# Sample cross attention on four column groups of the array: each head multiplied on its own 32 columns, one softmax over 128 rows

## The chip, the cores and the metric

The kernel runs on one core of a Trainium2 chip. The metric is the device time of one execution in microseconds. Before the change the median of three runs is 3585.67 us (3581.64 to 3586.48).

## What is computed

Two layers of a decoder trunk, for a prompt of 1024 tokens and for 8 samples of one new token each, which share the weights. In each layer a token mixer, a cross attention to 256 memory tokens and a gated MLP with a short convolution add to the residual. The change is in the cross attention of the samples. The prompt has keys and values that the layer computes; every sample has its own, from a cache in HBM:

```python
def cross_attention(h, mk, mv, w_xq_l, w_xo_l):
    q = (h @ w_xq_l).reshape(B, L, X_HEADS, X_HEAD_DIM)          # 4 heads of 256
    s = jnp.einsum('bqhd,bmhd->bhqm', q, mk) * (X_HEAD_DIM ** -0.5)
    p = jax.nn.softmax(s, axis=-1)
    o = jnp.einsum('bhqm,bmhd->bqhd', p, mv)
    return o.reshape(B, L, D_MODEL) @ w_xo_l
```

For the samples `h` is 8 x 1 x 1024, and `mk` and `mv` are 8 x 256 x 4 x 256 of float32: one MB of keys and one MB of values for each sample and layer.

## The kernel before, in words

Activations lie transposed, with features on the 128 partitions: `xT`, `Y`, `hh` and `hl` are 128 x 8 x 1032, the last 8 columns being the samples. Each weight slab (128 x 1024, 512 KB) is loaded into a ring of two buffers (`w_raw`), split by ScalarE into a high part (L235) and by GpSimd into the rest (L243), and kept in one of three places. A product with weights is three multiplications (L258 to L260). `stage_cross_ffn` writes every engine's order out by hand, and the engines meet at semaphores.

Cross attention has three stages on TensorE. The prompt's scores, turns and values come first, with the output projection of the first 384 columns, `unit(0, i)`. Then come `unit(1, 0)` to `unit(1, 7)`, the output projection of the next 384 columns, 24 multiplications of 384 columns each; the samples' attention lies between these. Then `unit(2, i)` takes the last 264 columns, which hold the 8 samples, so that `unit(2, 0)` waits for the samples' output (`s_lo`).

The samples' attention goes in this order.

- SyncE (`caches`, L2031) loads 16 pieces of one MB, t = 0 to 7 the keys and t = 8 to 15 the values of the samples, in turn into the two buffers `mem_keys` and `mem_values`. Piece t waits until TensorE is done with piece t-2 (`s_done`). After pieces 4, 6, 8, 10 and 12 it loads a weight slab.
- VectorE clears `probs` (L2497) and puts the samples' queries into it (L2499), with 32 columns for each sample and feature block, one of which isn't zero.
- `sample_scores(t)` (L2147) multiplies 8 feature blocks, 32 stationary columns and 256 moving columns, one after another into the same 32 rows (row 8h+b of bank 0, so that all heads and samples share 32 rows). Two samples follow each of `unit(1, 0)` to `unit(1, 3)`.
- Softmax over 32 rows: VectorE takes the maximum (L2507, L2508), ScalarE the exponential (L2345), VectorE clears the first 528 columns of `probs` (L2509) and divides (L2512, L2513). `unit(1, 4)` covers this. `sample_turn` (L2154) transposes the rows, VectorE copies them into `probs` (L2517), `unit(1, 5)` covers that.
- `sample_values(t)` (L2166) makes 4 multiplications of 512 moving columns into 32 rows of two banks. t = 8, 9, 10 come before `unit(1, 6)`, t = 11 to 15 after it, then `mean(1)` (L2110) and `unit(1, 7)`.
- ScalarE copies the 32 x 1024 result (L2353) beside `unit(1, 7)`, `sample_out` (L2174) turns it with 8 transposes, ScalarE and VectorE split it into high and low part (L2358, L2526), and `unit(2, 0)` goes on.

A float32 multiplication shows as two records in the trace, so L2147 has 256 records for 128 multiplications.

Elsewhere in the kernel smaller tiles of the array are used as well: the prompt's window attention puts its values (L485) on two groups of 64 columns in turn, and the samples' window attention (L1459) too.

Of the kernel before, what the change touches and what calls it, by code (L numbers as in the profile page):

```python
# [11 lines left out]
ALU = mybir.AluOpType  # L12
ACT = mybir.ActivationFunctionType
AX = mybir.AxisListType

P = 128
D = 1024
SEQ = 1024
NS = 8
T = SEQ + NS  # L20
# [3 lines left out]
KT = D // P  # L24
# [9 lines left out]
NMEM = 256  # L34
XH = 4
# [116 lines left out]
def build_program(nc, io):  # L152
    ctx = ExitStack()
    with ctx:
# [32 lines left out]
        Y = sb("Y", [P, KT, T])  # L187
# [3 lines left out]
        rs = sb("rs", [P, T])  # L191
        gT = sb("gT", [P, DEPTH, N_GROWS])
        cT = sb("cT", [P, DEPTH, 4, 2 * FT])
        ident = sb("ident", [P, P])
# [10 lines left out]
        ps = ctx.enter_context(nc.psum_tensor("ps", [P, 8, 512], F32))  # L205
# [6 lines left out]
        act_c, dve_c, pe_c, pool_c = (Chain(lasting_sem(n)) for n in ("act_step", "dve_step", "pe_step", "pool_step"))  # L212
# [1537 lines left out]
        def stage_cross_ffn(l, mkT, mv_tile, memory):  # L1750
# [6 lines left out]
            with ExitStack() as ph:  # L1757
                def tmp(name, shape, dt=F32):
                    return ph.enter_context(nc.sbuf_tensor(f"{name}{l}", shape, dt))

                probs = tmp("x_probsT", [P, KT * 264])
                acc, sq, rt = tmp("x_acc", [P, 2, 384]), tmp("x_sq", [P, 2, 384]), tmp("x_rt", [P, 2, 384])
                S = [t.rearrange("p (j k) -> p j k", j=2) for t in (rs[:, 0:512], rs[:, 512:1024], tmp("x_scores", [P, 512])[:])]
                small = tmp("x_small", [P, 4, 4, 2])
                rows, st = probs[0:32, 600:856], tmp("xs_stat", [32, 4])
                PT = probs[:, 0:2048].rearrange("p (a h q) -> p a h q", a=2, h=XH)
                qm = probs[:].rearrange("p (k c) -> p k c", k=KT)
                qm_at = probs[:].rearrange("p (k b c) -> p k b c", k=KT, b=NS)
                pm = probs[:, 0:528].rearrange("p (a c) -> p a c", a=2)
                pm_at = probs[:, 0:528].rearrange("p (a b c) -> p a b c", a=2, b=NS)[:, :, :, 0:32]\  # L1770
                    .rearrange("p a b (h e) -> p a b h e", e=8)[:, :, :, :, 0]
                o_rows = probs[0:32, 1024:2048]
                flat = [t[:].rearrange("p k t -> p (k t)") for t in (mkT, mv_tile)]
                mv = flat[1].rearrange("p (a f) -> p a f", a=2)
                s = {n: sem(f"x_{n}") for n in (
# [4 lines left out]
                scale = 256 ** -0.5  # L1780
# [35 lines left out]

                def new_values(bank):

                    t = ps[:, bank, 0:288].rearrange("p (h c) -> p h c", h=XH)[:, :, 0:64]
                    return t.rearrange("p h (d e) -> p h d e", d=2)[:, :, :, 0:NS]  # L1820

                def by_head(t):
                    return t.rearrange("p (h d) b -> p h d b", d=2)
# [20 lines left out]
                class End:  # L1844
# [7 lines left out]
                    s = {n: sem(f"e_{n}") for n in ("sq", "sum", "root", "x", "hh", "hl", "rs", "norm", "whole", "tree", "mean")}  # L1852
# [204 lines left out]
                def tensor(pe):  # L2057
# [32 lines left out]
                    def unit(c, i):  # L2090
                        u = KT * c + i
                        m = LOAD_OF[VISIT[l, "xo", xo_slab(u), c]]
                        wait_low(pe, m)
                        pe.wait_ge(s["out_lo"], (16, 24, 32)[c])
                        if c == 2:
                            pe.wait_ge(s["s_lo"], 1)
                        if u >= 2:
                            pe.wait_ge(s["out"], u - 1)
                        for j in range(KT):
                            w = slice(P * j, P * j + P)  # L2100
                            last = mm3(ps[:, 6 + u % 2, 0:C3[c][1]], w_hi[:, SLOT[m], w], w_lo[:, SLOT[m], w],
                                       hh[:, j, cols(c)], hl[:, j, cols(c)], j == 0, j == KT - 1)
                        last.then_inc(w_used, 1)
# [37 lines left out]
                    def sample_scores(t):  # L2141
                        if t == 0:
                            pe.wait_ge(s["q_ready"], 1)
                        pe.wait_ge(kv_in[t % 2], 16 * (t // 2 + 1))
                        keys = cache(t).rearrange("p (k t) -> p k t", k=KT)
                        for k in range(KT):
                            last = nc.tensor.matmul(ps[0:32, 0, 0:NMEM], qm[:, k, 32 * t:32 * t + 32], keys[:, k, :],  # L2147
                                                    start=(t == 0 and k == 0), stop=(t == NS - 1 and k == KT - 1))
                        last.then_inc(s["s_done"], 1)

                    def sample_turn():
                        pe.wait_ge(s["p_r"], 1)
                        for a in range(2):
                            last = nc.tensor.transpose(ps[:, 1, 32 * a:32 * a + 32], rows[:, P * a:P * a + P], ident[0:32, 0:32])  # L2154
                        last.then_inc(s["pT"], 1)

                    def sample_values(t):
                        b = t - NS
                        if b == 0:
                            pe.wait_ge(s["pm"], 1)  # L2160
                            pe.wait_ge(s["out_lo"], 32)
                        pe.wait_ge(kv_in[t % 2], 16 * (t // 2 + 1))
                        v = cache(t).rearrange("p (a f) -> p a f", a=2)
                        for a in range(2):
                            for h in range(2):
                                last = nc.tensor.matmul(ps[0:32, 4 + h, :], pm[:, a, 32 * b:32 * b + 32],  # L2166
                                                        v[:, a, 512 * h:512 * h + 512],
                                                        start=(b == 0 and a == 0), stop=(b == NS - 1 and a == 1))
                        last.then_inc(s["s_done"], 1)

                    def sample_out():
                        pe.wait_ge(s["o_rows"], 1)
                        for k in range(KT):
                            last = nc.tensor.transpose(ps[:, 1, 32 * k:32 * k + 32], o_rows[:, P * k:P * k + P], ident[0:32, 0:32])  # L2174
                        last.then_inc(s["o_turned"], 1)

                    for u in range(3):
# [16 lines left out]
                    unit(1, 4)  # L2194
                    sample_turn()
                    unit(1, 5)
                    for t in (8, 9, 10):
                        sample_values(t)
                    unit(1, 6)
                    for t in (11, 12, 13, 14, 15):  # L2200
                        sample_values(t)
                    mean(1)
                    unit(1, 7)
                    sample_out()
                    unit(2, 0)
                    mean(2)
# [41 lines left out]
                def scalar(act):  # L2248
# [79 lines left out]
                    for u in range(n):  # L2328
# [5 lines left out]
                        if u >= 9:  # L2334
# [7 lines left out]
                    high(0, range(KT))  # L2342
                    evacuate(1, 3)
                    act.wait_ge(s["neg_r"], 1)
                    nc.scalar.activation(rows[:], ps[0:32, 0, 0:NMEM], ACT.Exp, bias=st[:, 1:2], scale=scale,  # L2345
                                         accum_out=st[:, 2:3]).then_inc(s["exp_r"], 1)
                    squares(0, range(4))
                    evacuate(1, 4)
                    squares(0, range(4, KT))
                    evacuate(1, 5)  # L2350
                    evacuate(1, 6)
                    act.wait_ge(s["s_done"], 2 * NS)
                    nc.scalar.activation(o_rows.rearrange("p (h f) -> p h f", h=2), ps[0:32, 4:6, :], ACT.Copy)\  # L2353
                        .then_inc(s["o_rows"], 1)
                    root(1)
                    evacuate(1, 7)
                    act.wait_ge(s["o_turned"], 1)
                    nc.scalar.activation(by_head(hh[:, :, SEQ:T]), new_values(1), ACT.Copy).then_inc(s["s_hi"], 1)  # L2358
                    evacuate(2, 0)
# [53 lines left out]
                def vector(dve):  # L2413
# [81 lines left out]
                    add(("post", 0, KT - 1))  # L2495
                    dve.wait_ge(s["pv"], 32)
                    dve_c(nc.vector.memset(probs[:], 0.0))  # L2497
                    for h in range(XH):
                        last = nc.vector.tensor_copy(qm_at[:, 2 * h:2 * h + 2, :, 8 * h], Y[:, 2 * h:2 * h + 2, SEQ:T])  # L2499
                    last.then_inc(s["q_ready"], 1)  # L2500
                    normalise(0)
                    add(("post", 1, 1))
                    residual(0)
                    add(("post", 1, 2))
                    add(("post", 1, 3))
                    dve.wait_ge(s["s_done"], NS)
                    dve_c(nc.vector.tensor_reduce(st[:, 0:1], ps[0:32, 0, 0:NMEM], AX.X, ALU.max))  # L2507
                    nc.vector.tensor_scalar(st[:, 1:2], st[:, 0:1], -scale, None, ALU.mult).then_inc(s["neg_r"], 1)  # L2508
                    dve_c(nc.vector.memset(probs[:, 0:528], 0.0))  # L2509
                    low(0, range(0, 4))  # L2510
                    dve.wait_ge(s["exp_r"], 1)
                    dve_c(nc.vector.reciprocal(st[:, 3:4], st[:, 2:3]))  # L2512
                    nc.vector.tensor_scalar(rows[:], rows[:], st[:, 3:4], None, ALU.mult).then_inc(s["p_r"], 1)  # L2513
                    low(0, range(4, KT))
                    adds(0, range(1, 4))
                    dve.wait_ge(s["pT"], 1)
                    nc.vector.tensor_copy(pm_at, ps[:, 1, 0:64].rearrange("p (a h b) -> p a b h", a=2, h=XH))\  # L2517
                        .then_inc(s["pm"], 1)
                    add(("post", 1, 4))
                    adds(0, range(4, KT))  # L2520
# [263 lines left out]
```

## Time and profile before

| | us |
|---|---|
| median of three runs (lowest, highest) | 3585.67 (3581.64, 3586.48) |
| profiled execution, first to last instruction | 3580.1 |
| TensorE busy in it | 3358.2 (94%) |
| VectorE, ScalarE, GpSimd busy | 2316.4, 1186.1, 677.1 |
| mean granted TensorE clock | 0.985 |

For the profiled execution the profile gives the span alone and no separate time; it is 5.6 us below the median of the runs. The engine rows name a line, an engine, an operation and what it writes and reads. PE is TensorE's multiplication, PEld its weight load, DVE is VectorE, ACT ScalarE, POOL GpSimd, SPq the queue of SyncE that issues DMAs. Layer 0's cross attention lies at 820 to 1010 us, layer 1's some 1778 us later.

### The profile page before, as it was taken

What the parts mean: (1) busy time and instruction counts of PE and PEld (TensorE: products, weight loads), DVE (VectorE), ACT (ScalarE), POOL (GpSimd) and SP (SyncE); (2) the same over time, 40 slices, a digit from 0 to 9 for tenths busy, and PEclk for the clock granted to TensorE, in tenths of its full rate; (3) what the DMA queues carried; (4) which work ended last, traced back from release to release, by engine and by line L of the source; (5) the groups of instructions that cost most, each with busy time, mean ns of one, the idle gap of its engine ahead of it and who ended that gap; (6) DMA issues with size and microseconds to landing.
All of it is one profiled execution on the core that took longest, in us unless ns stands there. A gap on an engine that the chain in (4) does not pass through costs nothing. (4 is left out here: it accounts for less than half of the span.)

```text
span 3580.1 us, 50156 instructions
## 1 busy us (share of the span) xinstructions
PE 3358.2 (94%) x20988; PEld 3141.1 (88%) x20988; DVE 2316.4 (65%) x3517; ACT 1186.1 (33%) x1849; POOL 677.1 (19%) x274
## 2 busy tenths in 40 slices
PE   7999889899999999999989998898999999999997
PEld 7999769788599999999889997698876999999996
DVE  6766783733467677776786667736434777676776
ACT  5342363433332222212344324533433221222222
POOL 1111131012221212122111111211113121212120
PEclk9999999999999999999999999999999999999998
DMA  4111223203311111111121122322143111111111
GB/s 171 43 42 61 74 86 124 74 30 141 142 58 42 48 42 54 42 48 44 50 79 43 43 63 72 106 107 76 36 153 134 42 42 48 48 42 48 42 58 50
DMA packets 71168, 245.76 MB, mean 69 GB/s; under 512 B 7968, under 2 KB 22560, under 8 KB 65824
## 3 DMA queue, kind: packets, MB, share of 16 engines
q1 hardware_dynamic: 70656, 242.50, 19.9%
q8 instruction: 166, 2.72, 0.3%
q14 instruction: 58, 0.48, 0.0%
q10 hardware_dynamic: 288, 0.06, 0.0%
HBM read 214.20 MB, written 23.04 MB: 66 GB/s over the span
## 5 line engine op out<-in xcount | busy, mean ns | idle before, releaser
L258 PE MATMUL ps<-hh,w_hi 128*128 128x344 f32 (+2 forms) x4320 | 1417.5, 328 | 105.2 <-issue 26.1
L260 PE MATMUL ps<-hh,w_lo 128*128 128x344 f32 (+2 forms) x4320 | 1389.6, 322 | 0.0
L259 PE MATMUL ps<-hl,w_hi 128*128 128x344 f32 (+2 forms) x4320 | 1389.3, 322 | 0.0
L243 POOL TENSOR_TENSOR w_lo<-w_raw,w_hi 128x1024 fp32r<-128x1024 f32 x270 | 676.9, 2509 | 2840.4 <-ACT w_hi L235 2840.4
L258 PEld LDWEIGHTS ps<-hh,w_hi 128*128 128x128 f32 x4320 | 821.0, 190 | 142.9 <-issue 86.8
L259 PEld LDWEIGHTS ps<-hl,w_hi 128*128 128x128 f32 x4320 | 820.7, 190 | 3.0 <-issue 0.9
L260 PEld LDWEIGHTS ps<-hh,w_lo 128*128 128x128 f32 x4320 | 820.3, 190 | 0.0
L2581 DVE TENSOR_TENSOR Y<-Y,ps 128x344 f32<-128x344 f32 x912 | 432.9, 512 | 156.3 <-PE ps L260 156.3
L235 ACT ACTIVATE w_hi<-w_raw 128x1024 fp32r<-128x1024 f32 x296 | 310.3, 1052 | 438.4 <-PE ps L260 385.6
L2377 ACT ACTIVATE f_c<-f_u,cT 128x1032 f32<-128x1032 f32 (+1 forms) x92 | 111.3, 1212 | 670.0 <-DVE f_u L2546 663.4
L259 PE MATMUL ps<-f_glo,w_hi 128*128 128x344 f32 x960 | 308.1, 321 | 0.0
L260 PE MATMUL ps<-f_ghi,w_lo 128*128 128x344 f32 x960 | 307.6, 320 | 0.0
L258 PE MATMUL ps<-f_ghi,w_hi 128*128 128x344 f32 x960 | 306.1, 319 | 0.0
L2554 DVE SCALAR_TENSOR_TENSOR f_c<-f_u,cT,f_c 128x1024 f32<-128x1024 f32 x172 | 225.2, 1309 | 98.6 <-ACT f_c L2377 95.6
L258 PEld LDWEIGHTS ps<-f_ghi,w_hi 128*128 128x128 f32 x960 | 181.3, 189 | 0.0
L260 PEld LDWEIGHTS ps<-f_ghi,w_lo 128*128 128x128 f32 x960 | 180.6, 188 | 0.0
L259 PEld LDWEIGHTS ps<-f_glo,w_hi 128*128 128x128 f32 x960 | 180.3, 188 | 0.0
L2546 DVE TENSOR_TENSOR f_u<-ps,rs 128x1032 f32<-128x1032 f32 x86 | 105.7, 1229 | 98.8 <-PE ps L260 98.5
L2556 DVE SCALAR_TENSOR_TENSOR f_c<-f_cache,cT,f_c 128x8 f32<-128x8 f32 x172 | 123.6, 719 | 6.2
L1594 DVE TENSOR_TENSOR oq_acc<-oq_acc,oq_sq 128x384 f32<-128x384 f32 (+1 forms) x84 | 43.3, 515 | 96.7 <-ACT oq_sq L1519 92.2
L2393 ACT ACTIVATE f_ghi<-f_c 128x1032 fp32r<-128x1032 f32 x42 | 44.9, 1068 | 149.6 <-DVE f_c L2562 149.6
L258 PE MATMUL ps<-mem_hi,w_hi 128*128 128x256 f32 x256 | 76.7, 300 | 17.6 <-DVE mem_lo L634 10.5
(355 smaller groups left out, 3912.6 us busy)
## 6 DMA issues: line engine op xcount, KB each, us to landing
w_raw<-in_w_stream SPq DMA_DIRECT2D x296, 512.0 KB, 3.3
out_y_cols<-xT SPq DMA_DIRECT2D x9, 1376.0 KB, 5.7
xT<-out_y_cols SPq DMA_DIRECT2D x2, 4128.0 KB, 14.2
mem_keys<-in_cache_mem_k SPq DMA_DIRECT2D x8, 1024.0 KB, 4.8
mem_values<-in_cache_mem_k SPq DMA_DIRECT2D x8, 1024.0 KB, 4.9
mem_keys<-in_cache_mem_v SPq DMA_DIRECT2D x8, 1024.0 KB, 4.7
mem_values<-in_cache_mem_v SPq DMA_DIRECT2D x8, 1024.0 KB, 5.0
xT<-in_x_cols SPq DMA_DIRECT2D x3, 1376.0 KB, 11.5
```

The lines of the kernel that those rows point to most:

```text
L235: nc.scalar.activation(w_hi[:, SLOT[m], :], w_raw[:, m % RR, :], ACT.Copy).then_inc(hi_done, 1)
L243: nc.gpsimd.tensor_tensor(w_lo[:, SLOT[m], :], w_raw[:, m % RR, :], w_hi[:, SLOT[m], :].bitcast(F32), ALU.subtract).then_inc(lo_done["pool ...
L258: nc.tensor.matmul(out, whi, mhi, start=start, stop=False)
L259: nc.tensor.matmul(out, whi, mlo, start=False, stop=False)
L260: return nc.tensor.matmul(out, wlo, mhi, start=False, stop=stop)
L1594: nc.vector.tensor_tensor(a, a, sq[:, j % 2, 0:C3[c][1]], ALU.add).then_inc(acc_used, 1)
L2377: nc.scalar.activation(C[:, h, at], U[:, h, 2 + at.start:2 + at.stop], ACT.Identity, bias=cT[:, l, 3, col:col + 1], scale=cT[:, l, 2, col: ...
L2393: nc.scalar.activation(gh[:, j % 2, :], C[:, 1, :], ACT.Copy).then_inc(f_gh, 1)
L2546: nc.vector.tensor_tensor(tokens3(U[:, h, 2:2 + T]), ps[:, 3 * h:3 * h + 3, 0:CH], tokens3(rs[:]), ALU.mult).then_inc(f_up, 1)
L2554: dve_c(nc.vector.scalar_tensor_tensor(c[:, 0:SEQ], U[:, h, t:t + SEQ], w, c[:, 0:SEQ], ALU.mult, ALU.add))
L2556: dve_c(nc.vector.scalar_tensor_tensor(c[:, SEQ:T], ca[:, col, t, :], w, c[:, SEQ:T], ALU.mult, ALU.add))
L2581: nc.vector.tensor_tensor(y, y, b, ALU.add).then_inc(f_y, 1)
```

## The change

Each head gets its own 32 columns of the array and so its own 32 rows of PSUM. For the scores, the outer loop goes over the two feature blocks of a head (`d`) and the inner over the four heads, so that four multiplications in a row write to rows 0, 32, 64 and 96 of bank 0. Softmax is over 128 rows. Two transposes of 128 x 128 take the place of two of 32 x 128. For the values each head multiplies 256 columns (8 multiplications of 256 instead of 4 of 512) into its 32 rows of bank 4. The result is 128 x 256, `sample_out` is 2 transposes instead of 8. The zeros in `probs` are kept, so the second clearing falls away, and the queries are placed by one copy instead of four. The rows lie in `x_scores` instead of `probs`. The values are placed anew: t = 8, 9 after `unit(1, 5)`, 10, 11 after `unit(1, 6)`, then `mean(1)` and `unit(1, 7)`, then 12 to 15 and `sample_out` right behind them. ScalarE's copy of the result comes after `root(1)` and `evacuate(1, 7)`. The loads are as before.

```diff
+                rows, o_rows, st = third[:, 0:256], third[:, 256:512], tmp("xs_stat", [P, 4])
-                pm = probs[:, 0:528].rearrange("p (a c) -> p a c", a=2)
-                o_rows = probs[0:32, 1024:2048]
+                one_at = probs[:].rearrange("p (k b c) -> p k b c", k=KT, b=NS)[:, :, :, 0]
...
+                def sample_cols(k, b):
+                    return qm[:, k, 32 * b:32 * b + 32]
+                def head_rows(h):
+                    return slice(32 * h, 32 * h + 32)
...
-                        for k in range(KT):
-                            last = nc.tensor.matmul(ps[0:32, 0, 0:NMEM], qm[:, k, 32 * t:32 * t + 32], keys[:, k, :],
-                                                    start=(t == 0 and k == 0), stop=(t == NS - 1 and k == KT - 1))
+                        for d in range(2):
+                            for h in range(XH):
+                                k = 2 * h + d
+                                last = nc.tensor.matmul(ps[head_rows(h), 0, 0:NMEM], sample_cols(k, t), keys[:, k, :],
+                                                        start=(t == 0 and d == 0), stop=(t == NS - 1 and d == 1))
...
-                            last = nc.tensor.transpose(ps[:, 1, 32 * a:32 * a + 32], rows[:, P * a:P * a + P], ident[0:32, 0:32])
+                            last = nc.tensor.transpose(ps[:, 1, P * a:P * a + P], rows[:, P * a:P * a + P], ident[:])
...
                         for a in range(2):
-                            for h in range(2):
-                                last = nc.tensor.matmul(ps[0:32, 4 + h, :], pm[:, a, 32 * b:32 * b + 32],
-                                                        v[:, a, 512 * h:512 * h + 512],
+                            for h in range(XH):
+                                last = nc.tensor.matmul(ps[head_rows(h), 4, 0:256], sample_cols(XH * a + h, b),
+                                                        v[:, a, 256 * h:256 * h + 256],
                                                         start=(b == 0 and a == 0), stop=(b == NS - 1 and a == 1))
...
-                        for k in range(KT):
-                            last = nc.tensor.transpose(ps[:, 1, 32 * k:32 * k + 32], o_rows[:, P * k:P * k + P], ident[0:32, 0:32])
+                        for d in range(2):
+                            last = nc.tensor.transpose(ps[:, 1, P * d:P * d + P], o_rows[:, P * d:P * d + P], ident[:])
...
                     unit(1, 5)
-                    for t in (8, 9, 10):
-                        sample_values(t)
+                    sample_values(8)
+                    sample_values(9)
                     unit(1, 6)
-                    for t in (11, 12, 13, 14, 15):
-                        sample_values(t)
+                    sample_values(10)
+                    sample_values(11)
                     mean(1)
                     unit(1, 7)
+                    for t in (12, 13, 14, 15):
+                        sample_values(t)
                     sample_out()
...
                     evacuate(1, 6)
-                    act.wait_ge(s["s_done"], 2 * NS)
-                    nc.scalar.activation(o_rows.rearrange("p (h f) -> p h f", h=2), ps[0:32, 4:6, :], ACT.Copy)\
-                        .then_inc(s["o_rows"], 1)
                     root(1)
                     evacuate(1, 7)
+                    act.wait_ge(s["s_done"], 2 * NS)
+                    nc.scalar.activation(o_rows, ps[:, 4, 0:256], ACT.Copy).then_inc(s["o_rows"], 1)
...
-                    for h in range(XH):
-                        last = nc.vector.tensor_copy(qm_at[:, 2 * h:2 * h + 2, :, 8 * h], Y[:, 2 * h:2 * h + 2, SEQ:T])
-                    last.then_inc(s["q_ready"], 1)
+                    nc.vector.tensor_copy(one_at, Y[:, :, SEQ:T]).then_inc(s["q_ready"], 1)
...
-                    dve_c(nc.vector.memset(probs[:, 0:528], 0.0))
```

## Rows read from the trace of the kernel before

**Rows 1.** The page: span, busy time of each engine.
```profile
span 3580.1 us, 50156 instructions
PE 3358.2 (94%) x20988; PEld 3141.1 (88%) x20988; DVE 2316.4 (65%) x3517; ACT 1186.1 (33%) x1849; POOL 677.1 (19%) x274
```

**Rows 2.** Stretches, both layers: scores, then values to `unit(2, 0)`. Start:end, length, engines, clock, DMA.
```profile
860.41:901.68 41.27, 41.27 (x201) 26.18 (x200) 10.85 (x6) 14.39 (x22) 11.68 (x4) 1.00 0.59 216
901.68:954.42 52.74, 47.45 (x173) 24.37 (x173) 16.52 (x27) 11.98 (x23) 2.35 (x1) 1.00 0.47 176
2638.60:2679.90 41.30, 41.30 (x201) 26.18 (x200) 10.86 (x6) 14.63 (x23) 11.69 (x4) 1.00 0.59 217
2679.90:2732.86 52.96, 47.65 (x175) 24.32 (x173) 16.52 (x27) 11.98 (x23) 2.35 (x1) 1.00 0.47 176
```

**Rows 3.** TensorE in order of time, layer 0: start, length, line, tiles.
```profile
860.41 3.64 PE L2147 MATMUL ps<-mem_keys,x_probsT 128*32 128x256 f32 x16
863.89 3.62 PE L2147 MATMUL ps<-mem_values,x_probsT 128*32 128x256 f32 x16
867.44 0.44 PE L258 MATMUL ps<-hh,w_hi 128*128 128x384 f32 x1
...
871.56 0.33 PE L260 MATMUL ps<-hh,w_lo 128*128 128x384 f32 x1
871.83 3.64 PE L2147 MATMUL ps<-mem_keys,x_probsT 128*32 128x256 f32 x16
...
906.09 0.30 PE L2154 MATMUL ps<-ident,x_probsT 32*128 32x32 f32 x2
...
910.73 3.62 PE L2166 MATMUL ps<-mem_keys,x_probsT 128*32 128x512 f32 x8
...
919.13 3.62 PE L2166 MATMUL ps<-mem_keys,x_probsT 128*32 128x512 f32 x8 [1.35 <-DMA mem_keys<-in_cache_mem_v]
...
952.73 0.68 PE L2174 MATMUL ps<-ident,x_probsT 32*128 32x32 f32 x8
954.42 0.36 PE L258 MATMUL ps<-hh,w_hi 128*128 128x264 f32 x1 [1.02 <-DVE hl L2526]
```

**Rows 4.** TensorE in order of time: two groups of 64 columns used in turn.
```profile
438.23 1.08 PE L485 MATMUL ps<-xT,rs 128*64 128x256 f32 x8
578.67 1.10 PE L1459 MATMUL ps<-ws_probsT,ws_values 128*64 128x4 f32 x32
```

**Rows 5.** SyncE's queue, values of layer 0: issue, length of issue, what is loaded.
```profile
914.38 0.33 SPq L2031 DMA_DIRECT2D mem_keys<-in_cache_mem_v  x1
914.75 0.43 SPq L226 DMA_DIRECT2D w_raw<-in_w_stream  x1
```

**Rows 6.** A piece alone, issue to landing; and the stretch of three transfers queued.
```profile
DMA to landing us min/median/max: 4.7/4.7/5.0
899.30:906.40 7.10, 7.10 (x39) 5.45 (x37) 4.44 (x11) 1.80 (x5) 0.00 (x0) 1.00 0.94 367
```

**Rows 7.** VectorE and ScalarE in order of time: softmax and the end of the values.
```profile
901.79 0.41 DVE L2507 TENSOR_REDUCE xs_stat<-ps 32x1 f32<-32x256 f32 x1 [5.95 <-PE ps L2147]
902.44 0.50 DVE L2509 MEMSET x_probsT<- 128x528 f32 x1
905.28 0.34 DVE L2513 TENSOR_SCALAR x_probsT<-x_probsT,xs_stat 32x256 f32<-32x256 f32 x1
909.45 0.28 DVE L2517 COPY x_probsT<-ps 128x64 f32<-128x64 f32 x1
848.62 0.38 ACT L2274 ACTIVATE hh<-ps 128x256 fp32r<-128x256 f32 x1 [3.63 <-PE ps L2086]
```

**Rows 8.** TensorE's clock after a long wait, layer 0: stretch before, at, and behind it.
```profile
636.86 0.59 PE L258 MATMUL ps<-hh,w_hi 128*128 128x264 f32 x1 [5.38 <-DVE w_lo L252]
635.40:642.00 6.60, 5.14 (x23) 5.14 (x24) 5.35 (x9) 1.73 (x3) 0.00 (x0) 0.50 0.32 96
918.00:953.00 35.00, 30.94 (x103) 13.87 (x103) 2.83 (x2) 4.01 (x6) 0.00 (x0) 1.00 0.50 186
```

More of the change, by code:

```diff
@@ L1762, in stage_cross_ffn @@
                 acc, sq, rt = tmp("x_acc", [P, 2, 384]), tmp("x_sq", [P, 2, 384]), tmp("x_rt", [P, 2, 384])
-                S = [t.rearrange("p (j k) -> p j k", j=2) for t in (rs[:, 0:512], rs[:, 512:1024], tmp("x_scores", [P, 512])[:])]
+                third = tmp("x_scores", [P, 512])
+                S = [t.rearrange("p (j k) -> p j k", j=2) for t in (rs[:, 0:512], rs[:, 512:1024], third[:])]
                 small = tmp("x_small", [P, 4, 4, 2])
-                rows, st = probs[0:32, 600:856], tmp("xs_stat", [32, 4])
+                rows, o_rows, st = third[:, 0:256], third[:, 256:512], tmp("xs_stat", [P, 4])
                 PT = probs[:, 0:2048].rearrange("p (a h q) -> p a h q", a=2, h=XH)
                 qm = probs[:].rearrange("p (k c) -> p k c", k=KT)
-                qm_at = probs[:].rearrange("p (k b c) -> p k b c", k=KT, b=NS)
-                pm = probs[:, 0:528].rearrange("p (a c) -> p a c", a=2)
-                pm_at = probs[:, 0:528].rearrange("p (a b c) -> p a b c", a=2, b=NS)[:, :, :, 0:32]\
-                    .rearrange("p a b (h e) -> p a b h e", e=8)[:, :, :, :, 0]
-                o_rows = probs[0:32, 1024:2048]
+                one_at = probs[:].rearrange("p (k b c) -> p k b c", k=KT, b=NS)[:, :, :, 0]
                 flat = [t[:].rearrange("p k t -> p (k t)") for t in (mkT, mv_tile)]
@@ L1817, in new_values @@
                 def new_values(bank):
-                    t = ps[:, bank, 0:288].rearrange("p (h c) -> p h c", h=XH)[:, :, 0:64]
-                    return t.rearrange("p h (d e) -> p h d e", d=2)[:, :, :, 0:NS]
+                    return ps[:, bank, 0:256].rearrange("p (d h c) -> p h d c", d=2, h=XH)[:, :, :, 0:NS]
+                def sample_cols(k, b):
+                    return qm[:, k, 32 * b:32 * b + 32]
+                def head_rows(h):
+                    return slice(32 * h, 32 * h + 32)
                 def by_head(t):
@@ L2344, in scalar @@
                     act.wait_ge(s["neg_r"], 1)
-                    nc.scalar.activation(rows[:], ps[0:32, 0, 0:NMEM], ACT.Exp, bias=st[:, 1:2], scale=scale,
+                    nc.scalar.activation(rows, ps[:, 0, 0:NMEM], ACT.Exp, bias=st[:, 1:2], scale=scale,
                                          accum_out=st[:, 2:3]).then_inc(s["exp_r"], 1)
@@ L2506, in vector @@
                     dve.wait_ge(s["s_done"], NS)
-                    dve_c(nc.vector.tensor_reduce(st[:, 0:1], ps[0:32, 0, 0:NMEM], AX.X, ALU.max))
+                    dve_c(nc.vector.tensor_reduce(st[:, 0:1], ps[:, 0, 0:NMEM], AX.X, ALU.max))
                     nc.vector.tensor_scalar(st[:, 1:2], st[:, 0:1], -scale, None, ALU.mult).then_inc(s["neg_r"], 1)
-                    dve_c(nc.vector.memset(probs[:, 0:528], 0.0))
                     low(0, range(0, 4))
@@ L2512, in vector @@
                     dve_c(nc.vector.reciprocal(st[:, 3:4], st[:, 2:3]))
-                    nc.vector.tensor_scalar(rows[:], rows[:], st[:, 3:4], None, ALU.mult).then_inc(s["p_r"], 1)
+                    nc.vector.tensor_scalar(rows, rows, st[:, 3:4], None, ALU.mult).then_inc(s["p_r"], 1)
                     low(0, range(4, KT))
@@ L2516, in vector @@
                     dve.wait_ge(s["pT"], 1)
-                    nc.vector.tensor_copy(pm_at, ps[:, 1, 0:64].rearrange("p (a h b) -> p a b h", a=2, h=XH))\
+                    nc.vector.tensor_copy(one_at, ps[:, 1, 0:256].rearrange("p (k c) -> p k c", k=KT)[:, :, 0:NS])\
                         .then_inc(s["pm"], 1)
```

## The prediction, made before the changed kernel ran

> **What bounds the kernel now.** I read the page first: TensorE is busy for 94% of the span, VectorE for 65%, the others far less [rows 1]. So the time is that of TensorE's queue, and the change is worth what it takes out of that queue less the waits it puts in. Next the two stretches of each layer that the change touches [rows 2]: from the end of `mean(0)` to the end of the scores 41.3 us, from there to `unit(2, 0)` 52.7 and 53.0 us, 94.0 us a layer. In the first TensorE is never idle, and the DMA engines are already busy for 0.59 of it; keep that share in mind. TensorE's order of time shows the pieces [rows 3]: a pair of samples takes 867.44 - 860.41 = 7.03 us, one sample 3.48 us, which is 16 records of 0.217 us; a unit between them takes 871.83 - 867.44 = 4.39 us. A sample's values take the same 3.46 us, and three loads are waited for, 1.4 us each (one of them is shown).
>
> **Do column groups run side by side?** No row has four groups. The nearest has two: L485 puts 8 records, also of 256 columns, on two groups of 64 in 1.08 us [rows 4]. A last record lasts 0.40 us (3.64 - 15 x 0.216), so one after another they would take 7 x 0.216 + 0.40 = 1.91 us, and two at a time 3 x 0.216 + 0.40 = 1.05 us. It is two at a time, with nothing lost. Four at a time would be 4 x 0.216 + three small starts, some 0.89 us a sample; no gain over two is the other end, 1.73; no overlap at all 3.46. Can records be issued so fast? 0.89 us asks for one each 0.055 us, and L1459 shows 32 in 1.10 us, 0.034 each [rows 4]. I take 0.89, the step of L485 repeated.
>
> The Trainium skill, "TensorE: Matmul & The Clock Gate", Part 3, speaks against this change: it has weight loads run beside multiplications in flight only where the row groups differ, and here all four tiles span all rows. By that rule each of the four rounds of a sample would also pay its weight load (a rival below). The 1.08 us of L485, whose tiles also span all rows, leaves no room for such loads, so the trace disagrees.
>
> **What then ends last: the loads.** By TensorE's work alone 16 samples would shrink from 55.5 to 14.2 us, a gain of 41 us a layer. But piece t+2 is issued only when sample t is done. A lone piece lands 4.7 us after its issue [rows 6]. The queue gives 2.6 MB (two pieces and a slab) in 7.1 us [rows 6], so a piece queued behind another adds about 2.65 us and a slab 1.3. Two pieces and a slab are due for every unit and pair, and TensorE's part of that round would be 4.39 + 1.8 = 6.2 us: the DMA engines become the bound there, at 7 to 7.5 us a round against 11.4 before.
>
> **The walk**, in us from the end of `mean(0)`, with the issue 0.2 us after a sample is done (910.73 + 3.46 = 914.19, issued 914.38, the slab right behind) [rows 3, 5]. Piece 1 is there at the start. Scores: samples 0, 1 done at 0.9, 1.8; piece 3 lands at 7.7 (TensorE waits 0.6), sample 3 done 8.6; piece 5 lands 16.0 (wait 2.0), done 16.9; piece 7 lands 22.6 (wait 0.4), done 23.5. So the scores end at 23.6, not 41.3. `unit(1, 4)`, the turn at 0.3 and `unit(1, 5)` follow, values 8, 9 are done at 34.5. `unit(1, 6)`, value 10 at 39.7; piece 11 lands at 42.4 (wait 2.7), done 43.3. `mean(1)`, `unit(1, 7)`, then 12, 13 at 49.1 and 50.0. Now nothing covers the loads: piece 14, issued 49.3, lands at 53.9 (wait 4.0), piece 15 lands at 56.6 (wait 1.8), done 57.5. The loads take back about 11.5 us a layer, where they took 4.3.
>
> **The end of the values.** Before, the copy out of PSUM ran under `unit(1, 7)`, and 1.69 us lay between that unit and `unit(2, 0)` [rows 3]. Now TensorE waits for the copy: 0.2 until the last multiplication has ended, 0.4 for a copy of 128 x 256 [L2274, rows 7], 0.4 for two transposes, then the same 1.0 us of high and low part: 2.0 us, so `unit(2, 0)` starts at 59.5. The same walk with 3.48 us a sample and the old order gives 93.3 where the trace has 94.0; I add that 0.7: 60.2. The gain is 94.0 - 60.2 = 33.8 us a layer.
>
> **The clock.** A wait of 5.38 us was followed by a stretch at 0.50 of the clock, 1.2 GHz; in it 264-column records came each 0.22 us instead of 0.12, and 23 of them lost 2.3 us [rows 8]. Waits of 1.4 us beside samples kept 1.00 (918 to 953) [rows 8]. The new end has waits of 4.0, 1.8 and 2.0 us in 10 us, so I charge one such stretch, 2.0 us a layer; the ends are nothing and two of them, 4.6.
>
> **What costs nothing.** The softmax must be done within `unit(1, 4)`, 4.4 us. It took from 901.79 to 905.62, and 128 rows cost as 32 do, since columns set the time; the clearing of 0.50 us goes [rows 7]. It has 0.5 us to spare before and 1.0 after; without that cover TensorE would wait for the chain itself, 3.8 us. VectorE's copy of the turned rows (909.45 to 909.73) had 1.0 us of cover before 910.73 and keeps it. The queries' placing, one copy instead of four, lies before `mean(0)` ends. ScalarE's `root(1)` and `evacuate(1, 7)` now come before its wait for the samples, which helps: behind that wait only the copy and its successors queue. On SyncE's queue slabs come between pieces as before; GpSimd works 11.7 of 41.3 us and has room in 23.6 [rows 2]. From `unit(2, 0)` on every load and split hangs on TensorE's own progress, so the rest moves up as it is.
>
> **Sum.** (33.8 - 2.0) x 2 layers = 63.6 us. 3580.1 - 63.6 = 3516.5 by the profiled execution; the median of the runs lies 5.6 us higher: **3522 us**.
>
> **Rivals.**
> - Two at a time at best, because four streams of moving data are too many. 1.73 us a sample: the same walk ends at 68.2 with waits of 3.1 and 0.9 us, gain 25.8, less 1 us of clock: 3585.7 - 49.6 = 3536. Speaks for it: nothing beyond two is shown. Chance 0.09.
> - Weight loads not hidden: with the four groups running in step, each round of four would first wait for its weights. A step from full tiles to 32 columns, which has a load in the open, loses 0.09 us [rows 3]; with 0.11 a sample takes 4 x (0.216 + 0.11) = 1.30 us, the walk ends at 64.3, gain 29.7 less 2.0: 3585.7 - 55.4 = 3530. L485 speaks against it. Chance 0.05. This is what the rule of the Trainium skill above would do here.
> - The groups don't overlap at all, so the change does not do what it says: 3.46 us a sample, only the new placing of the values is left, the walk ends at 91.3, two layers gain 5: 3580. Chance 0.03.
> - Slower: TensorE drains at each change of column group. Going from full tiles to 32 columns costs 871.83 - 871.56 = 0.27 us against a step of (871.56 - 867.44) / 23 = 0.18, so 0.09 is lost [rows 3]; with 256 records a layer that is 23 us on top of 91.3, 20.3 us more than before in each layer: 3626. It decides from (94.0 - 91.3) / 256 = 0.01 us a change. L485 changes group with every multiplication and loses nothing. Chance 0.03.
>
> **How the numbers follow.** The forecast has 0.80. Its own range: with a piece queued at 2.4 us instead of 2.65 and no clock loss the gain is 36 us a layer, 3514; with 3.0 us and 4.6 of clock, 30.5 - 4.6 = 25.9, 3534. Rounded outwards for the additions of the walk, and reaching over the two nearer rivals: 3511 to 3541. What can be told from no change is 0.2%, 7 us. Faster: 0.80 + 0.09 + 0.05 = 0.94; same 0.03; slower 0.03.
>
> **What would show it right.** L2147 with four records that start almost together, a pair under 2 us; TensorE's waits then named as loads of pieces 3, 5, 7, 11, 14 and 15, some 11 us a layer; DMA near 0.9 busy in the scores; `unit(2, 0)` about 60 us after `mean(0)`; half clock near it. If samples take over 1.2 us, a group limit is at work. If the span falls by under 45 us with 0.9 us a sample, the loads or the clock were sized wrong. A wait before `sample_turn` would say that the softmax's cover is gone.

## The result, and the profile after

The changed kernel takes 3540.94 us (median of four, 3539.99 to 3543.64) beside 3583.7 us for the kernel before on the same chip: a ratio of 0.9882, 95% interval 0.9868 to 0.9896, so 1.2% or 42 us less, where 64 us were forecast. Taken against the 3585.67 us of the forecast, the ratio gives 3543 us, just above the range. The direction and the mechanism were right; the gain forecast was half as large again as the one measured. The same kernel in a second set came to 0.9870 (0.9853 to 0.9886).

The page of the changed kernel (the lines that answer to [rows 1]):

```profile
span 3539.5 us, 50378 instructions
PE 3302.3 (93%) x21104; PEld 3132.6 (89%) x21104; DVE 2323.0 (66%) x3509; ACT 1186.1 (34%) x1849; POOL 676.7 (19%) x274
```

The stretches of the stage, from the end of `mean(0)` to `unit(2, 0)`: the scores of layer 0, the rest of layer 0, then both for layer 1. Columns as in [rows 2]; the last three numbers are the granted clock, the busy share of the DMA engines and GB/s:

```profile
867.06:893.90 26.84, 22.04 (x201) 16.07 (x200) 12.94 (x6) 14.40 (x22) 11.38 (x4) 0.96 0.91 343
893.90:935.30 41.40, 32.22 (x235) 24.17 (x231) 16.08 (x26) 11.48 (x23) 2.42 (x1) 0.83 0.58 215
2622.70:2650.00 27.30, 22.61 (x201) 17.44 (x200) 12.93 (x6) 13.01 (x21) 9.13 (x3) 0.94 0.78 299
2650.00:2689.55 39.55, 30.26 (x236) 22.07 (x231) 17.76 (x26) 13.02 (x25) 4.77 (x2) 0.88 0.66 253
```

The stage takes 68.2 us in layer 0 and 66.9 in layer 1 instead of 94.0; without the clock's share I had walked to 60.2, with it to 62.2. The DMA engines, at 0.59 of the scores' time before, are at 0.91 in layer 0 and 0.78 in layer 1: the loads have become the limit there. The clock, which was 1.00 throughout, is down to 0.83 in the second stretch.

TensorE in order of time, layer 0 (the lines that answer to [rows 3]):

```profile
867.06 1.07 PE L2152 MATMUL ps<-mem_keys,x_probsT 128*32 128x256 f32 x16
867.95 1.05 PE L2152 MATMUL ps<-mem_values,x_probsT 128*32 128x256 f32 x16
873.39 1.07 PE L2152 MATMUL ps<-mem_keys,x_probsT 128*32 128x256 f32 x16
875.87 1.07 PE L2152 MATMUL ps<-mem_values,x_probsT 128*32 128x256 f32 x16 [1.40 <-DMA mem_values<-in_cache_mem_k]
...
892.20 1.93 PE L2152 MATMUL ps<-mem_values,x_probsT 128*32 128x256 f32 x16 [2.60 <-DMA mem_values<-in_cache_mem_k]
...
915.20 1.61 PE L2171 MATMUL ps<-mem_values,x_probsT 128*32 128x256 f32 x16 [2.69 <-DMA mem_values<-in_cache_mem_v]
...
928.86 1.61 PE L2171 MATMUL ps<-mem_keys,x_probsT 128*32 128x256 f32 x16 [4.08 <-DMA mem_keys<-in_cache_mem_v]
931.30 1.93 PE L2171 MATMUL ps<-mem_values,x_probsT 128*32 128x256 f32 x16 [0.84 <-DMA mem_values<-in_cache_mem_v]
933.74 0.69 PE L2179 MATMUL ps<-ident,x_scores 128*128 128x128 f32 x2 [0.51 <-ACT x_scores L2362]
935.30 0.56 PE L258 MATMUL ps<-hh,w_hi 128*128 128x264 f32 x1 [0.87 <-DVE hl L2529]
```

A sample starts 0.89 us behind the one before it (867.95 - 867.06): four column groups do run side by side. In layer 0 the waits stand where the walk put them, before pieces 3, 5, 7, 11, 14 and 15 (1.4, 0.8, 2.6, 2.7, 4.1 and 0.8 us). In layer 1 there is none before piece 7; the one before piece 5 is 2.7 us instead, and one of 0.7 us stands before piece 4. But at 892.20 and 931.30 a sample lasts 1.93 us. There TensorE runs at half clock. The stretches at 0.50, 1.2 GHz, in the order of time; the second, for comparison, lies between two of them:

```profile
891.80:898.40 6.60, 6.20 (x30) 4.93 (x31) 4.12 (x11) 1.85 (x6) 1.17 (x1) 0.50 0.91 346
898.60:904.80 6.20, 6.20 (x37) 6.02 (x36) 4.87 (x8) 3.26 (x6) 2.08 (x1) 1.00 0.04 15
915.70:918.90 3.20, 3.20 (x17) 1.77 (x10) 0.00 (x0) 0.47 (x1) 0.00 (x0) 0.50 0.91 317
929.30:939.40 10.10, 7.89 (x49) 5.23 (x42) 0.23 (x1) 0.61 (x2) 0.00 (x0) 0.50 0.13 54
956.60:959.90 3.30, 3.30 (x17) 3.30 (x16) 3.30 (x4) 1.63 (x4) 2.24 (x1) 0.50 0.52 169
```

Four of them in and behind the stage of one layer, where I had charged one. Layer 1 has four too. In layer 0 the first three come with the waits of 2.6, 2.7 and 4.1 us, at their end or right behind it.

### The profile page after: what moved, and what is told of

The parts are those of the page before. It is cut to its first block and busy times, and to the rows that moved or that the text cites. A ratio compares the mean times of both kernels' runs of the same rounds, so it can differ in the third digit from the quotient of the medians.

```text
span 3539.5 us, 50378 instructions
## 1 busy us (share of the span) xinstructions
PE 3302.3 (93%) x21104; PEld 3132.6 (89%) x21104; DVE 2323.0 (66%) x3509; ACT 1186.1 (34%) x1849; POOL 676.7 (19%) x274
## 5 line engine op out<-in xcount | busy, mean ns | idle before, releaser
L1117 DVE TENSOR_TENSOR Y<-ps,rs 128x344 f32<-128x344 f32 x120 | 59.9, 509 | 53.5 <-PE ps L260 53.3
```

The source lines that it names most:

```text
L1117: nc.vector.tensor_tensor(dst[:, cols(c)], ps[:, u % 3, 0:CH], rs[:, cols(c)], ALU.mult)\
```

## The experiments

Ratios are to the kernel before in the same set of runs, with the 95% interval. us of two kernels are compared within one set.

**The changed kernel again, as a control.**

> The changed kernel once more, as a control. In its first profile the stretch from the end of mean(0) to unit(2, 0) takes 68.2 us in layer 0 where 60.2 were forecast, and the kernel reaches mean(0) 6.65 us later than the kernel before although nothing is changed there. Theory A (TensorE's clock falls to half after the waits for loads, and that is where the forecast's gain went): the half-clock stretches within this stage come again at the same places, near the waits for pieces 7, 11 and 14. The 6.65 us ahead of it: if they come from where the low-clock stretches happen to fall, they differ in this profile (anything from 0 to 7 us); if the change causes them, they are 6 to 7 us again. Time 3541 us, within 3.

3537.13 us, 0.9870 (0.9853 to 0.9886). The low stretches come again in the stage, 13.3 and 13.7 us of half clock in the two layers after 16.3 and 12.7 in the first profile. `mean(0)` ends at 865.8 us, 5.4 later than in the kernel before; see the last section for that. The stage's two lengths:

```profile
865.80:932.70 66.90, 53.14 (x432) 39.36 (x431) 28.99 (x32) 26.06 (x45) 14.21 (x5) 0.90 0.71 272
2622.10:2689.60 67.50, 53.94 (x431) 39.91 (x431) 30.58 (x32) 25.99 (x45) 13.54 (x5) 0.90 0.71 268
```

**TensorE kept busy in the waits.**

```diff
+                    def warm(n):
+                        for _ in range(n):
+                            nc.tensor.matmul(ps[:, 2, 0:P], ones[:], ident[:], start=True, stop=True)
...
+                        warm({3: 5, 5: 3, 7: 9}.get(t, 0))
                         pe.wait_ge(kv_in[t % 2], 16 * (t // 2 + 1))
```

> TensorE multiplies a constant by a constant (128 x 128, float32, into a bank that nobody reads then) in the waits: 5, 3, 9 times before the scores of t = 3, 5, 7; 9, 16, 5 times before the values of t = 11, 14, 15; 3 and 4 times around sample_out. All results stay. Theory A (clock): the low-clock stretches of the stage vanish or shrink to one, units in it run at 4.4 us again, the stage falls from 68 to 60 to 63 us, and the kernel gains 8 to 16 us over the changed one: 3525 to 3533 us. Theory B (the loads are slower than forecast and the clock hurts little because its stretches lie in waits): no gain, 3539 to 3545 us.

3529.69 us, 0.9850 (0.9836 to 0.9865), 7.4 us less than the changed kernel in the same set, although it does more work. Both stages ran at full clock:

```profile
864.10:927.60 63.50, 61.20 (x540) 49.38 (x539) 28.96 (x32) 26.09 (x45) 14.10 (x5) 1.00 0.75 286
2613.50:2679.90 66.40, 60.95 (x540) 49.49 (x539) 28.97 (x32) 25.95 (x45) 13.69 (x5) 1.00 0.72 273
```

The stages are 129.9 us together against 134.4, so 4.5 us of the gain lie in them; from the end of the first to the start of the second it is 1685.9 us against 1689.5 in the control, where low stretches reach into the units behind the stage. The time lies in theory A's range, but the gain is just below its 8 to 16 us: with the clock at 1.00 the stage still takes 63.5 and 66.4 us, not 60.2. TensorE's order of time in layer 0 shows why, samples 7 and 11 and `unit(2, 0)`; the stage starts at 864.10:

```profile
889.40 1.07 PE L2157 MATMUL ps<-mem_values,x_probsT 128*32 128x256 f32 x16 [0.46 <-DMA mem_values<-in_cache_mem_k]
909.61 1.07 PE L2177 MATMUL ps<-mem_values,x_probsT 128*32 128x256 f32 x16 [0.85 <-DMA mem_values<-in_cache_mem_v]
927.59 0.36 PE L258 MATMUL ps<-hh,w_hi 128*128 128x264 f32 x1
```

Piece 7 is used at 25.3 us of the stage and piece 11 at 45.5, both still waited for behind the fillers, where the walk had 22.6 and 42.4. So the loads are late at full clock too. In layer 1 the fillers before piece 7 outlast its landing by 1.5 us; in layer 0 none outlasts its piece by more than 0.3.

**No loads.**

```diff
                     for t in range(2, 2 * NS):
-                        caches(t)
+                        sp.wait_ge(s["s_done"], t - 1)
...
-                        pe.wait_ge(kv_in[t % 2], 16 * (t // 2 + 1))
+                        pe.wait_ge(kv_in[t % 2], 16)
```

> Of the 16 pieces only t = 0 and 1 are loaded, and all samples read these two, so the samples' attention is computed from the wrong keys and values; SyncE's waits stay, the other 14 MB per layer are left out. No wait for a piece can occur. Theory A and B both give the stage without load waits: 7 units of 4.39, 16 samples of 0.89, the turn, mean(1) and 2 us at the end, 48 to 49 us a layer and no low clock, so 19 to 20 us less than the changed kernel in each layer: 3500 to 3504 us. If samples also read slower without loads or the softmax is late, 3508 or more. The difference to the changed kernel is the whole price of the loads, waits and clock together.

3497.70 us, 0.9764 (0.9749 to 0.9778): 39.4 us less than the changed kernel.

```profile
864.20:914.10 49.90, 47.01 (x432) 37.48 (x431) 33.13 (x32) 25.84 (x45) 15.37 (x5) 1.00 0.21 70
2598.70:2648.50 49.80, 46.99 (x432) 37.47 (x431) 33.14 (x32) 25.82 (x45) 15.21 (x5) 1.00 0.20 69
```

No low clock, and a stage of 49.9 us where TensorE's own work had been put at 48 to 49; a wait for the softmax of 1.6 us makes the difference. Loads, with all that they bring, cost the changed kernel 17 to 18 us in each stage; the forecast had 13.5, of them 11.5 for waits and 2.0 for the clock.

**Heads outside.**

```diff
-                        for d in range(2):
-                            for h in range(XH):
-                                k = 2 * h + d
+                        for h in range(XH):
+                            for d in range(2):
+                                k = 2 * h + d
```

> The two loops of the scores and of the values are exchanged: heads outside, the two halves of the contraction inside, so two multiplications in a row go to the same 32 columns before the next head. The same work and results. If TensorE starts multiplications strictly in order, only the second half of one head runs beside the first of the next: a sample takes 1.3 to 1.8 us instead of 0.89, TensorE's own work in the stage rises by 7 to 14 us a layer, partly inside the waits for loads: 3546 to 3560 us. If each column group works off its own queue, the order doesn't matter: 0.89 us, 3541 us.

3536.28 us, 0.9871 (0.9857 to 0.9886): no difference. A sample is 0.89 us here too:

```profile
859.25 1.09 PE L2152 MATMUL ps<-mem_keys,x_probsT 128*32 128x256 f32 x16
860.14 1.08 PE L2152 MATMUL ps<-mem_values,x_probsT 128*32 128x256 f32 x16
```

So the four groups fill even where two multiplications in a row go to the same one, and the expectation's theory of a strict order falls.

**The old places, with column groups.** The edit puts t = 8 to 10 and 11 to 15 and ScalarE's copy back where they were.

> Column groups as in the change, but the values where they were before: t = 8, 9, 10 after unit(1, 5), 11 to 15 after unit(1, 6), and ScalarE's copy of the result beside unit(1, 7). With 0.89 us a sample the first bunch now waits some 4 us for piece 10, the second waits for 12, 13, 14 and 15: about 13 us of waits for loads in the values instead of 7.6, less the 2 us end that unit(1, 7) hides again. If placement matters as the walk says, the stage is 2 to 4 us longer than the changed kernel's 67: 3541 to 3546 us. If the waits bring more low clock than the changed kernel has, up to 3552. If placement did nothing, 3537.

3544.77 us, 0.9893 (0.9878 to 0.9908). The stage takes 72.8 and 73.4 us at a clock of 0.86 and 0.84:

```profile
860.50:933.30 72.80, 55.14 (x431) 41.04 (x430) 28.95 (x32) 25.91 (x45) 13.95 (x5) 0.86 0.66 250
```

Placement is worth some 6 us a stage in the profile, more than the walk's 2 to 4; more of the stage runs at half clock too, 20.5 and 23.9 us against 13.3 and 13.7 in the control. In the ratios it is 0.001 to 0.002 (0.9893 beside 0.9882 and 0.9870), a few us of the whole, and the intervals overlap: in the profiled execution the way to layer 0's stage was 5.2 us shorter than in the control's.

**The new places alone.** The same edit on the kernel before, the other way round.

> The kernel before, with only the new placing of the values and of ScalarE's copy; all heads still share 32 columns and 32 rows. The walk gives 91.3 us for the stage instead of 94.0: two of the three 1.4 us waits for loads go, but the result's copy (1.0 us), 8 transposes and the two parts now stand in TensorE's way. My forecast had 5 us less in two layers, 3578 us; the theory that placement costs more than it gives without the column groups has 3584 to 3587.

3582.65 us, 0.9998 (0.9989 to 1.0008). The stage is 91.8 us in both layers where the walk had 91.3; right behind it a stretch at low clock takes the 2.2 us back:

```profile
860.90:952.70 91.80, 88.62 (x374) 50.63 (x373) 27.42 (x33) 26.47 (x45) 14.03 (x5) 1.00 0.52 198
952.70:956.50 3.80, 3.80 (x19) 3.80 (x20) 0.00 (x0) 0.00 (x0) 0.00 (x0) 0.55 0.02 4
```

Three waits of 1.3, 1.1 and 0.8 us, with work between, stood before that. So the new places alone bring nothing; the column groups alone, in the old places, bring 0.9893, and both 0.9870 to 0.9882.

**The slabs behind the odd pieces.**

```diff
-                        if t in (4, 6, 8):
+                        if t in (5, 7, 9):
                             load_slabs(sp, first + t // 2 + 1)
-                        if t in (10, 12):
-                            load_slabs(sp, second + t // 2 - 4)
+                    load_slabs(sp, second + 2)
```

> The changed kernel with the weight slabs moved in SyncE's queue: behind pieces 5, 7 and 9 instead of between 4 and 5, 6 and 7, 8 and 9, and the last two behind piece 15 instead of between 10 and 11, 12 and 13. Same bytes. Theory A: a slab of 512 KB ahead of the odd piece costs its 1.3 us in the wait for pieces 5, 7, 11: these waits (0.8, 2.6, 2.7 us) fall to 0, 1.3 and 1.4, a low-clock stretch or two go with them, the stage falls by 4 to 7 us: 3523 to 3530 us against 3537 to 3541. Theory B: the DMA engines are saturated over the whole stage, so the bytes only move to the next wait: 3535 to 3540.

3528.75 us, 0.9845 (0.9830 to 0.9860). The stage is 3 to 5 us shorter than the control's 66.9 and 67.5:

```profile
864.20:927.90 63.70, 50.88 (x432) 38.47 (x431) 31.14 (x32) 26.00 (x45) 14.17 (x5) 0.93 0.75 285
2615.80:2678.50 62.70, 50.31 (x432) 37.20 (x431) 31.12 (x32) 25.96 (x45) 14.20 (x5) 0.93 0.78 289
```

As expected, the waits before pieces 5, 7 and 11 fall in layer 0, to 0, 1.4 and 2.0 us. The scores end there after 23.9 us, and now `sample_turn` waits 1.1 us for the softmax. ScalarE, in order of time, shows what stands before the exponential:

```profile
888.37 1.06 ACT L235 ACTIVATE w_hi<-w_raw 128x1024 fp32r<-128x1024 f32 x1 [2.21 <-DMA w_raw<-in_w_stream]
889.44 1.28 ACT L2351 ACT_TABLE_LOAD   x1
890.74 0.48 ACT L2351 ACTIVATE x_scores<-ps,xs_stat 128x256 f32<-128x256 f32 x1
```

VectorE has the maxima at 888.87. But the slab that was moved behind piece 7 lands only at 888.3, ScalarE splits it first, and its table load of 1.28 us comes after that; in the changed kernel both were done when the scores ended, and ScalarE waited 3.0 us for VectorE. The kernel without loads has the same order, and its 1.6 us.

**Values in the middle of units.** `unit(1, 5)`, `(1, 6)` and `(1, 7)` make the multiplications of t = 8, 10 and 12 after half of their own; VectorE's copy of the turned rows goes ahead of four `low` and three `add` steps.

```diff
                         for j in range(KT):
+                            if j == KT // 2 and middle is not None:
+                                sample_values(middle)
```

> The changed kernel with the values of t = 8, 10 and 12 in the middle of unit(1, 5), (1, 6) and (1, 7), after half of its 24 multiplications, and VectorE's copy of the turned rows ahead of four low and three add steps. If the waits for pieces 14 and 15 are there because both are issued behind the last unit (one issue to landing, 4.7 us, in the open), then piece 14 is now issued 2.2 us before that unit ends and its wait falls from 4.1 to 2 us, the wait for piece 11 from 2.7 to about 2: stage shorter by 3 to 5 us, 3529 to 3534 us. If TensorE's changes between 128 and 32 columns cost much (0.1 to 0.3 us for each of the six), 3537.

3531.75 us, 0.9849 (0.9833 to 0.9866). The gain is there, but not by the waits as I had put it: in layer 0 the wait for piece 11 went from 2.7 to 0.4 us, and that for 14 grew from 4.1 to 5.0; in layer 1 it is 1.4, and the one for 15 is 2.8. Pieces 10 to 13 are used earlier and the loads don't come faster.

**Fillers at the end alone.** `warm` before t = 14, 15 and around `sample_out` only.

> The changed kernel with constant multiplications only in the waits at the end of the stage (16 and 5 times before the values of t = 14, 15; 3 and 4 times around sample_out), none in the earlier waits. It tells which waits cost the clock. My forecast charged one low stretch, at the end. If the end is all of it, the low stretch at 61 to 72 us of the stage goes, those at 18 to 30 and 48 us stay, and the time is that of the kernel with all the fillers, 3529 to 3531 us. If the earlier waits for pieces 7 and 11 cost as much, it is half way, 3532 to 3535.

3529.23 us, 0.9836 (0.9821 to 0.9852), as good as with all fillers. The stage's length hardly changes:

```profile
863.40:931.10 67.70, 59.08 (x488) 46.46 (x487) 28.98 (x32) 26.02 (x45) 14.09 (x5) 0.92 0.70 268
2617.70:2683.40 65.70, 57.72 (x487) 45.56 (x487) 28.99 (x32) 26.00 (x45) 13.82 (x5) 0.95 0.72 276
```

The low stretches in the middle stay (26 to 30 us and 47 to 54 us after the stage's start in layer 0, 26 to 30 and 47 to 50 in layer 1); the one at the end goes, and with it what it took from `unit(2, 0)` and the unit behind it. What the low clock in the middle of the stage costs is not clear of the noise in the times, though the stages are 3.5 us longer than with all fillers; partly it ran in time in which the next load was on its way anyhow.

**Slabs and fillers; slabs and halves; all three.**

> The slabs behind the odd pieces and the fillers in all waits (5, 5 before the scores of 3, 7; 3 before the turn; 5, 16, 5 before the values of 11, 14, 15; 3, 4 around the end). Theory A holds load waits and clock for two costs that add: the slabs gave 8.4 us, the fillers 7.4, so 3519 to 3524 us, with no low stretch in the stage. If the slabs' gain was mostly the clock's, the two overlap: 3525 to 3529.

> The slabs behind the odd pieces and the values of 8, 10, 12 in the middle of their units, no fillers. The slabs gave 8.4 us against the changed kernel, the halves 5.4. If both shorten different waits (slabs: those before pieces 5, 7, 11; halves: those before 11, 14), most of it adds: 3523 to 3527 us. If the DMA queue is the limit over the whole stage, 3527 to 3530.

> The same with fillers (5, 5 before the scores of 3, 7; 3 before the turn; 10, 5 before the values of 14, 15; 3, 4 around the end). The floor is the kernel without loads, 3497.7 us; DMA alone needs 14 pieces of 3.1 to 3.4 us and a few slabs, some 50 us of the stage, plus 3 us at its end. Expected: stage 57 to 60 us without low clock, 3513 to 3519 us. If fillers cost more than they save once the waits are short: no better than without them.

| | us | ratio (95% interval) | stages, us |
|---|---|---|---|
| slabs and fillers | 3521.62 | 0.9819 (0.9805 to 0.9833) | 61.6, 61.8 |
| slabs and halves | 3520.96 | 0.9821 (0.9806 to 0.9836) | 59.6, 60.0 |
| all three | 3514.81 | 0.9800 (0.9787 to 0.9814) | 61.0, 58.0 |

The costs add, within the intervals: the changed kernel stands at 0.9870 and 0.9882, slabs bring it to 0.9845, slabs and halves to 0.9821, fillers on top to 0.9800. That one beats both kernels, the kernel before by 2.0%, by 72 us. Its stages, all at full clock:

```profile
868.00:929.00 61.00, 57.31 (x501) 44.87 (x500) 31.23 (x32) 25.98 (x45) 14.11 (x5) 1.00 0.81 298
2612.70:2670.70 58.00, 57.15 (x502) 44.89 (x501) 31.25 (x32) 25.95 (x45) 15.59 (x5) 1.00 0.83 312
```

## Why the prediction was right in kind and wrong in size

- **Four groups side by side: right.** 0.89 us a sample was forecast from L485's two groups, 0.89 was measured. The rivals with 1.73, 1.30 and 3.46 us a sample and the drain are out. The rule of the Trainium skill, "TensorE: Matmul & The Clock Gate", Part 3, that weight loads overlap only where row groups differ, would have given 1.30 us here; the run disagrees, as L485 did.
- **The loads end last: right, but sized too small; the first term of the sum that failed.** The walk had 11.5 us of waits a layer and a stage of 60.2 us without the clock's share. With the clock at 1.00 (fillers) the stages take 63.5 and 66.4 us, 9.5 us more in two layers, of which up to 2 may be fillers that outlast a load. In the changed kernel piece 7, forecast for 22.6 us, was used at 25.1. About half of that comes from piece 3. The prediction has it land at 7.7 us, though its own costs give 1.1 + 4.7 + 2.65 = 8.4, and it landed at 8.8, which moves everything behind it. The rest is the load of piece 7: it landed 7.9 us after its issue, 3.6 behind the slab ahead of it. The other pieces that were queued in the scores landed 2.5 us behind what was ahead of them, so the cost of 2.65 was right for them, although [rows 6] (1.05 MB at 367 GB/s) would give 2.9. Why piece 7 took longer, and in layer 1 piece 4 (7.4 us from issue to landing where layer 0 has 4.8), stays open. GB/s in 40 equal slices from 867 to 900 us show that the DMA engines don't stream evenly: between one round of loads and the next there is a dip.

```profile
GB/s 417 412 268 149 397 407 457 417 417 159 169 238 437 402 382 477 417 417 238 99 129 397 457 353 422 467 407 387 159 189 417 447 338 392 194 248 437 298 99 40
```

- **The clock: the second term that failed.** "I charge one such stretch, 2.0 us a layer". The profile has four stretches a layer, 24 and 20 us long by the trace's records with what lies behind the stage, 16.3 and 12.7 us of it in the stage. I had read [rows 8] as: 5.4 us of waiting brings it, 1.4 us doesn't. The walk itself had waits of 2.0 and 2.7 us, which lie between, and I let them pass; [rows 8] had no row for them. In layer 0 the way from the scores' end to the first values, one turn and two units, took 11.0 us instead of 9.1, with half clock at its start, and the values and their end 30.4 instead of 27.5. Behind the stage `unit(2, 0)` and following ran at 0.22 us a record instead of 0.12, which I hadn't counted at all: 3.0 us more between the stage and layer 1's stage than before, and 2.7 after that (5.1 and 0 in the control). What the low clock costs, though, is less than what it stretches. TensorE's busy time in the stage is 54.3 and 52.9 us, where it is 47.0 without loads; but the fillers gave 7.4 us back in two layers, where 4.0 were charged, since the loads are awaited at full clock too.
- **The sum.** 63.6 us forecast, 40.6 in the profiled execution. The stages are 135.1 us together instead of the 124.4 forecast with the clock: 10.7 us. The low clock behind them: 5.7. The way to layer 0's stage, which the change doesn't touch, was 6.7 us longer in this execution. That makes the 23.0, but for rounding. Of these the first two belong to the kernel, the last to the execution. The median lies only 1.4 us above the profiled span, not the 5.6 that the forecast added, so of the 64 us some 19 to 21 are missing in the runs. Within the control's set it is 17.3 (46.3 instead of 63.6): the loads with all that they bring cost 39.4 us instead of 27.0, which is 12.4 of it, and the other 5 are missing without loads too, 1.2 us in each stage and the rest outside them.
- **Softmax, copies, SyncE's queue, the end of the values: right.** The chain is as long with 128 rows as with 32 (0.43 us for the maximum, 0.41 before), and its cover of 4.4 us sufficed; it doesn't where ScalarE comes late to the exponential (slabs behind the odd pieces, no loads). The copy of the result and the two parts cost 0.5 and 0.9 us of waits in the open, as forecast.
- **The new places.** 2.7 us a layer was forecast for them on the old multiplications and 2.2 measured in the stage; behind it low clock takes them back, 2.0 and 2.2 us in the two layers. That was the clock term's failure once more, in small.

## What to carry to other kernels

When TensorE's work in a stage shrinks to a quarter, write down the loads' timetable before the gain: with two buffers each load waits for the use of the last but one, so the order in the DMA queue (weights behind the piece that is awaited) and an even spread of the uses gave 0.5% on top of the change's 1.2%. And charge the waits twice: once for their length, and once for the clock, where they are as long as the 2.6 to 4.1 us here, also in the units that follow. Constant multiplications in the waits gave 7.4 us back, and those at the stage's end alone did as well (0.9836 beside 0.9850).

## What the runs showed of the hardware

**Column groups fill by themselves.** With the heads outside, two multiplications in a row for the same 32 columns, the trace still shows four records starting within 0.04 us of each other and the next four 0.2 us later; with the heads inside the four start within 0.02 us. A record doesn't name its column group. The order of the program among the groups did not matter for 256 columns of float32.

**The same code takes up to 9 us more or less before the stage, mostly by the clock.** Up to the end of `mean(0)` all these kernels are the same, and the stretch took 859.3 us in one profile and 868.0 in another. TensorE's busy time in it rises with the length of its stretches at low clock, at the same count of instructions but for a few records. The kernel before, the changed one, the one with the heads outside, and the one with all three edits:

```profile
0.00:860.40 860.40, 782.11 (x5088) 728.33 (x5088) 533.69 (x855) 363.32 (x638) 142.74 (x63) 0.98 0.23 79
0.00:867.00 867.00, 791.22 (x5088) 734.71 (x5088) 535.00 (x852) 363.28 (x638) 142.94 (x63) 0.97 0.23 78
0.00:859.30 859.30, 781.65 (x5092) 727.24 (x5094) 535.77 (x852) 363.19 (x638) 143.29 (x63) 0.98 0.24 79
0.00:868.00 868.00, 791.21 (x5088) 734.88 (x5088) 535.16 (x852) 363.39 (x638) 142.98 (x63) 0.97 0.23 78
```

By the trace's clock records they ran 31, 48, 27 and 48 us of it at half clock. The clock isn't all: the control and the kernel with values in the middle of units both ran 37.5 us at half clock there, with the same busy time to 0.6 us, and differ by 3.1 us.

```profile
0.00:865.80 865.80, 785.58 (x5092) 732.23 (x5093) 534.88 (x852) 363.25 (x638) 143.21 (x63) 0.98 0.23 78
0.00:862.70 862.70, 786.14 (x5088) 732.66 (x5088) 535.64 (x852) 363.29 (x638) 143.15 (x63) 0.98 0.24 78
```

Why the same waits bring the low clock in one execution and not in the next stays open. For a change of 40 us it is a sixth of the effect in a single profile, and the reason to compare stretches between landmarks and not whole spans.
